# Where the sub-sequence order of dilated attention is made: in the copy out of PSUM, or in TensorE's reads

## The reference, cut to what matters

```python
ATT_GROUPS = ((128, 1), (512, 4), (2048, 16))      # window, dilation; 8 heads of 64 each
q_b = rms_norm(heads(q_b), attn_q_norm_w)          # over each head's 64 numbers
k_b = rms_norm(heads(k_b), attn_k_norm_w)

def dilated_window_attention(q, k, v, slopes, dilation, radius):
    sub = s // dilation
    def to_sub(a):                                  # token s*dilation + d -> sub-sequence d, place s
        return a.reshape(b, sub, dilation, h, dh).transpose(0, 2, 3, 1, 4)
    ...
    scores = einsum('bdhnqe,bdhnke->bdhnqk', qs, kw) * dh ** -0.5
    scores = scores - slopes * (rel * dilation)     # |q - k| <= 64 places of the sub-sequence
    o = einsum('bdhnqk,bdhnke->bdhnqe', exp(scores - lse), vw)
```

## Time and profile before

| | |
|---|---|
| median of 3 runs | 3678.52 us (3667.72 to 3679.44) |
| profiled execution, first to last instruction | 3676.7 us |
| TensorE busy | 3490.7 us, 95% |
| VectorE, ScalarE, GpSimd busy | 1486.8, 1033.1, 1346.8 us |
| attention passes 1 to 11 (79.9 to 744.8 us) | 664.9 us |

### The profile page before, as it was taken

One profiled execution on the slowest core, in us unless ns is written; L12 is line 12 of the kernel. 1 busy time (PEld: TensorE's weight loads), 2 busy tenths in 40 slices (PEclk: granted clock), 3 DMA queues, 4 the chain that ended last, 5 costly groups with the idle time before them and its releaser, 6 DMA issues. The chain is left out here.

```text
span 3676.7 us, 45201 instructions
## 1 busy us (share of the span) xinstructions
PE 3490.7 (95%) x17736; PEld 2874.7 (78%) x17736; DVE 1486.8 (40%) x2252; ACT 1033.1 (28%) x1749; POOL 1346.8 (37%) x1164
## 2 busy tenths in 40 slices
PE   6999999999989898989999999999899999999998
PEld 5777777776778887888778788788678887777877
DVE  4232323244254444444772333333444124444443
ACT  3343434341234343431121111111222124442221
POOL 4121222123342424232443333333342446544543
PEclk9999999999999899989999999999999999999999
DMA  2000000010210101012411111111231111111122
GB/s 102 23 30 24 29 26 28 28 33 29 88 45 19 46 24 45 19 44 85 149 53 53 51 46 46 46 46 51 69 118 44 52 46 49 44 44 52 57 86 75
DMA packets 104033, 187.69 MB, mean 51 GB/s; under 512 B 32313, under 2 KB 64697, under 8 KB 101185
## 3 DMA queue, kind: packets, MB, share of 16 engines
q1 hardware_dynamic: 103872, 185.48, 15.9%
HBM read 158.33 MB, written 27.12 MB: 50 GB/s over the span
## 5 line engine op out<-in xcount | busy, mean ns | idle before, releaser
L303 PE MATMUL DP<-XH,WH 128*128 128x512 f32 x2608 | 897.2, 425 | 23.7 <-POOL WL L251 23.7
L249 POOL CAST WH<-WRAW 128x1024 fp32r<-128x1024 f32 (+2 forms) x257 | 264.6, 1030 | 1647.1 <-issue 1026.1
L303 PE MATMUL DP<-XL,WH 128*128 128x512 f32 x2608 | 813.0, 393 | 0.0
L303 PE MATMUL DP<-XH,WL 128*128 128x512 f32 x2608 | 811.6, 393 | 0.0
L303 PEld LDWEIGHTS DP<-XH,WH 128*128 128x128 f32 x2608 | 475.3, 191 | 182.6 <-issue 85.6
L251 POOL TENSOR_TENSOR WL<-WRAW,WH 128x1024 fp32r<-128x1024 f32 (+2 forms) x257 | 587.3, 2285 | 20.7
L303 PEld LDWEIGHTS DP<-XL,WH 128*128 128x128 f32 x2608 | 494.9, 190 | 107.4
L303 PEld LDWEIGHTS DP<-XH,WL 128*128 128x128 f32 x2608 | 493.2, 189 | 107.2
L838 DVE SCALAR_TENSOR_TENSOR SS<-B,RQ,SBI 128x256 f32<-128x256 f32 (+2 forms) x192 | 74.5, 429 | 380.7 <-PE B L543 380.7
L688 ACT ACTIVATE PP<-SS,NM 128x256 f32<-128x256 f32 (+2 forms) x192 | 88.5, 461 | 317.5 <-DVE NM L845 317.5
L367 DVE TENSOR_TENSOR XR<-XR,B 128x1024 f32<-128x1024 f32 x88 | 106.5, 1219 | 101.5 <-PE B L347 101.5
(11 more groups left out here) (469 smaller groups left out, 5316.0 us busy)
## 6 DMA issues: line engine op xcount, KB each, us to landing
WRAW<-in_w_up SPq DMA_DIRECT2D x44, 512.0 KB, 3.5
WRAW<-in_w_attn SPq DMA_DIRECT2D x36, 512.0 KB, 3.5
WRAW<-in_w_down SPq DMA_DIRECT2D x22, 512.0 KB, 3.5
XR<-in_x SPq DMA_DIRECT2D x8, 1024.0 KB, 8.6
WRAW<-in_w_dn SPq DMA_DIRECT2D x16, 512.0 KB, 3.4
aa_dram<-AA SPq DMA_DIRECT2D x12, 512.0 KB
YY<-yy_dram SPq DMA_DIRECT2D x12, 512.0 KB, 4.1
WRAW<-in_w_lrux SPq DMA_DIRECT2D x10, 512.0 KB, 3.5
```

The costliest lines, as they stand in the source:

```text
L249: pool.tensor_copy(WH[b.slot][:, 0:b.kt, :], WRAW[b.slot][:, 0:b.kt, :]).then_inc(w_hi, 1)
L303: mm = pe.matmul(DP[b.slot][:, half * H:half * H + H], w[b.slot][:, k, :], x[:, k, half * H:half * H + H], start=one, stop=end)
```

## The change

The copies out of PSUM read with the step and write in a row, for the groups 1 and 2; TensorE then reads plain slices of 128 or 256 columns. `value_view` goes away; `att_tokens` stays for the outputs (L850), which are still written back in the order of tokens.

```diff
+        def tile(a, t):
+            return a[:, P * t:P * t + P]
+        def sub_order(g, a):
+            r = (1, 4, 8)[g]
+            return a.rearrange("p (s d) -> p d s", d=r) if g else a
+        def in_order(g, a):
+            r = (1, 4, 8)[g]
+            return a.rearrange("p (d s) -> p d s", d=r) if g else a
         def key_view(g, t, kz):
...
-                return kz[:, :, :].rearrange("p h (s d) -> p d h s", d=4)[:, t // 2], 256, 0 if t % 2 else 128
-            return kz[:, :, :].rearrange("p h (s d) -> p d h s", d=8)[:, t], P, 0
+                return kz[:, :, 256 * (t // 2):256 * (t // 2) + 256], 256, 0 if t % 2 else 128
+            return kz[:, :, P * t:P * t + P], P, 0
...  # scores
-                pe.matmul(SPS[t % 2]..., att_tokens(g, t)(QA[i % 2][:, :]),
+                pe.matmul(SPS[t % 2]..., tile(QA[i % 2], t),
...  # turn_v
-                    tr = pe.transpose(DP[...][:, P * j:P * j + P], value_view(i % NG, j), IDENT)
+                    tr = pe.transpose(DP[...][:, P * j:P * j + P], tile(VR, j), IDENT)
...  # square_sums
-                    sq = ASQ[:, P * t:P * t + P] if pos else att_tokens(i % NG, t)(ASQ[:, :])
+                    mm = pe.matmul(SUMS[:, o:o + 2], tile(ASQ, t), BLK[:, 0:P:64], start=True, stop=True)
...  # take_v
-                    cp = act.activation(VR[:, to:to + n], DP[b.slot][:, at_:at_ + n], ACT.Copy)
+                    cp = act.activation(in_order(g, VR[:, to:to + n]), sub_order(g, DP[b.slot][:, at_:at_ + n]), ACT.Copy)
...  # take_q
-                act.activation(ASQ[:, :], DP[b.slot][:, :], ACT.Square)
-                act.activation(QA[i % 2][:, :], DP[b.slot][:, :], ACT.Copy, scale=col("qn"))
+                act.activation(in_order(g, ASQ[:, :]), sub_order(g, DP[b.slot][:, :]), ACT.Square)
+                act.activation(in_order(g, QA[i % 2][:, :]), sub_order(g, DP[b.slot][:, :]), ACT.Copy, scale=col("qn"))
...  # take_k: the same for ASQ, and for each head
-                    cp = act.activation(KZA[i % 2][r, h, :], DP[b.slot][r, :], ACT.Copy,
+                    cp = act.activation(in_order(g, KZA[i % 2][r, h, :]), sub_order(g, DP[b.slot][r, :]), ACT.Copy,
```

More of the change, by code:

```diff
@@ L503, in value_chunks @@
             return [(t, 0)]
[L505 to L511, removed]
         def gate_block(m):
@@ L542, in scores @@
                 keys, w, _ = key_view(g, t, KZA[i % 2])
-                pe.matmul(SPS[t % 2][:, 0:2 * w].rearrange("p (h k) -> p h k", h=2), att_tokens(g, t)(QA[i % 2][:, :]),
+                pe.matmul(SPS[t % 2][:, 0:2 * w].rearrange("p (h k) -> p h k", h=2), tile(QA[i % 2], t),
                           keys, start=True, stop=True).then_inc(s_ready, 1)
@@ L580, in turn_v @@
                 for j in range(NT):
-                    tr = pe.transpose(DP[att_block(i, 2).slot][:, P * j:P * j + P], value_view(i % NG, j), IDENT)
+                    tr = pe.transpose(DP[att_block(i, 2).slot][:, P * j:P * j + P], tile(VR, j), IDENT)
                 tr.then_inc(vt_ready, 1)
@@ L591, in square_sums @@
                     o = 16 * pos + 2 * t
-                    sq = ASQ[:, P * t:P * t + P] if pos else att_tokens(i % NG, t)(ASQ[:, :])
-                    mm = pe.matmul(SUMS[:, o:o + 2], sq, BLK[:, 0:P:64], start=True, stop=True)
+                    mm = pe.matmul(SUMS[:, o:o + 2], tile(ASQ, t), BLK[:, 0:P:64], start=True, stop=True)
                 mm.then_inc(sums_done, 1)
@@ L704, in take_v @@
                 act.wait_ge(mm_done, b.n + 1)
-                moves = [(0, 0, T)] if i % NG else [(0, 64, 896), (896, 0, 64), (960, 960, 64)]
+                g = i % NG
+                moves = [(0, 0, T)] if g else [(0, 64, 896), (896, 0, 64), (960, 960, 64)]
                 for to, at_, n in moves:
-                    cp = act.activation(VR[:, to:to + n], DP[b.slot][:, at_:at_ + n], ACT.Copy)
+                    cp = act.activation(in_order(g, VR[:, to:to + n]), sub_order(g, DP[b.slot][:, at_:at_ + n]),
+                                        ACT.Copy)
                 cp.then_inc(vr_ready, 1)
@@ L730, in take_q @@
                     act.wait_ge(spread_ready, i)
-                act.activation(ASQ[:, :], DP[b.slot][:, :], ACT.Square).then_inc(asq_ready, 1)
-                act.activation(QA[i % 2][:, :], DP[b.slot][:, :], ACT.Copy, scale=col("qn")).then_inc(qa_ready, 1)
+                g = i % NG
+                act.activation(in_order(g, ASQ[:, :]), sub_order(g, DP[b.slot][:, :]), ACT.Square).then_inc(asq_ready, 1)
+                act.activation(in_order(g, QA[i % 2][:, :]), sub_order(g, DP[b.slot][:, :]), ACT.Copy,
+                               scale=col("qn")).then_inc(qa_ready, 1)
                 act.wait_ge(qa_ready, i + 1)
```

## The result

The changed kernel takes 3609.25 us (median of 4 runs, 3605.72 to 3632.88) against 3678.98 us before (4 runs, 3667.72 to 3682.15): the ratio is 0.9827, 95% interval 0.9808 to 0.9847, so 1.7% faster, clear of no change. The forecast was 3610 us. The profiled execution went from a span of 3676.7 to 3608.8 us.

What follows compares the result with a forecast made beforehand. TensorE, busy 3490.7 of 3676.7 us, was taken as the bound. Terms 28.2 + 13.7 + 15.9 + 10.3 = 68.1 us gave 3608.6, so a median of 3610 us; own range 3600 to 3618, 8 in 10 range 3598 to 3643.

Steps and rivals of the forecast that it cites:

- Scores: TensorE's scores steps with streaming keys unstrided: 0.95 us per tile in group 1, 0.49 in group 2; 28.2 and 13.7 us.
- Tile 0: Start of `turn` after the scores: some 5.05 us in group 1, gaining 0.40 us each; nothing gained in group 2.
- Squares and clock: Squares of the queries at j = 11 and 12: 15.9 us from unstrided weight loads, plus 10.3 us of clock.
- the 10.3 us: Time lost to TensorE's lower clock at j = 11 and 12 in eight passes, all expected back; rival of falls staying: 0.12.
- Copies: ScalarE's strided PSUM reads in `take_q`, `take_k`, `take_v`: nothing extra taken; the other bound was twice the time.
- The bound on its other side: Rival: strided PSUM copies cost double, TensorE waits ahead of `values` of tiles 2 and 5; 30 us back, 3640 us, chance 0.22.
- the prediction's reading of it for ScalarE: The skill's rule on non-contiguous PSUM access, read for ScalarE, is the doubled copy case: some 3640 us.
- Sum: Whole kernel: 68.1 us off 3676.7 us, so 3608.6 us for the profiled execution and 3610 us for the median.
- nothing keeps its own time: After the passes: `gateb` blocks, statistics and mixing all start from TensorE; weights' DMAs have 17 us and more per block.

Runs made afterwards that it cites:

- e3: Kernel before with only the keys (and their squares) in sub-sequence order; queries, squares of the queries and values as before: 3655.01 us, ratio 0.9950.
- e4: Kernel before with only the queries, as weights, in sub-sequence order; keys still stepped: 3675.86 us, ratio 0.9997.
- e2: Kernel before with only the squares of the queries in sub-sequence order; keys, queries and values as before: 3645.97 us, ratio 0.9924.
- e5: Changed kernel with the squares of the queries again written in token order and read with a step: 3654.58 us, ratio 0.9936.
- e1: Changed kernel with the step moved to the other end of the ScalarE copies (PSUM read in a row, SBUF written stepped): 3647.19 us, ratio 0.9925.
- e6_again: Changed kernel with two added waits on GpSimd, so its weight splits wait for the negated maximum of tiles 0 and 5: 3598.05 us, ratio 0.9784.

## Why the prediction was right

*Scores.* Right in both sizes: 0.95 us per tile in group 1, and 0.48 for 0.49 in group 2. Tile 0 too: 4.94, 5.03 and 4.81 us against 4.94, 5.05 and 4.81; the place where gain turns into a gap was read off group 0, which ran ahead of the others already. e3 and e4 show that it is the keys alone. The prediction called the weights of the groups the same, but the queries were read with a step in group 1 too: groups differ in keys and queries at once, and the rows before could not separate them. That it didn't matter was seen only in e3 and e4.

*Squares and clock.* 26.2 us forecast, 25.9 measured. That the clock's falls hang on the squares was argued from the passes without one; e2 and e5 show it from both sides. What the 10.3 us were is less firm than it looked. They are what 34 us at the lower clock cost while in every second of the eight passes the scores behind the squares were stepped and lost nothing to it; with all scores in a row the same squares cost 14 us of clock (e3, also 34 us at the lower level) and 18 (e5, 44 us). The prediction took the clock's price as a term of its own, and it hangs on the scores' term. Had the change been made in two parts, the sum of the parts would have come out otherwise than the whole: keys alone give 33 us in the passes, squares alone 26, both 64 with queries and values.

*Copies.* The value taken (nothing extra) was right, to 3 ns of 1026. It was the one term without a row: a choice between two bounds, with a chance of 0.22 left to the other. The argument for it, that both slow accesses in the rows were of SBUF, named the end that e1 shows to be the slow one, but no row had shown it. The bound on its other side has been made real by e1: 25 us of waits at the places named, and some 10 us of clock that the bound didn't have. With the step on the write side the kernel takes 38 us more by the medians (3647 for 3609; the prediction had 30, and 3640). The Trainium skill, PSUM — Partial Sum Buffer, Specifications (TRN2), says that any non-contiguous access slows matmuls; it doesn't speak of ScalarE, and the prediction's reading of it for ScalarE has not come true: for ScalarE's reads of float32 with a step of 16 or 32 bytes the rows above show that nothing slows, and the measurement decides. What PSUM does with a step in a matmul's output no run here shows.

*Sum.* The forecast of 3608.6 us for the profiled execution met 3608.8, and that is partly luck. Passes 1 to 12 gave 67.9 us where 68.1 was said. But after them the spreads took 6.4 us more (60.35 for 53.97) and the stages behind gave 6.6 back, and two other profiles of the same program have spans of 3600.1 and 3612.1 us. The prediction said that after the passes nothing keeps its own time; the clock in the spreads does. I had put the scatter of 12 us down as the range of three runs and not asked where it is made: between the three profiles of the changed kernel the one stretch of 50 us differs by 11 us and all behind it by 3.5. The thirteen runs of the changed kernel span 35 us (3597.71 to 3632.88), so that one execution met the forecast to 0.2 us says nothing about its steps; the pieces above do.

## What to carry to other kernels

Where float32 data have to be put in another order on their way out of PSUM, try it first in ScalarE's read: with a step of 4 or 8 floats it was free there (1026 ns), and cost double in ScalarE's write to SBUF (2032 ns) and in what TensorE streams (1.96 us for 1.02). In TensorE's weight loads the same step cost nothing beside a long stream (e4) and double where only two columns streamed (3.79 us for 1.84). VectorE and other types were not tried. A small matmul that is bound by its weight loads costs twice if it also pulls the clock down: look at the granted clock behind each such group before a gain is priced, and at the work that lies under the lower clock, since some of it loses nothing. And compare pieces of the same work between profiles before comparing whole kernels: the passes of the changed kernel repeat to 0.1 us where the kernel scatters by 35.

## What the runs showed that I had not expected

Twelve steps of a `gateb` k-tile and a spread with 8 rows take 3.49 us each at the full clock and 6.57 at the lower one, and between 3 and 68 us of them ran at the lower one, in the same program 3 and 27 us. The clock came back by itself, with the same spreads still running, in eleven of the twelve profiles; in e6_again it stayed down until the last of them. What sets the length of the stretch stays open. In the passes of e1 the clock fell behind the gap of 2.2 us in six of eight passes, while gaps of about 1 us, there and in tile 0 of the other kernels, were not followed by a fall.
